# Last row block in quarter-width groups, with a variance about the first half's mean and one quarter centred on GpSimd

## What is computed

```python
def layer_norm(x, g, b):
    xf = x.astype(jnp.float32)
    mu = jnp.mean(xf, -1, keepdims=True)
    var = jnp.mean(jnp.square(xf - mu), -1, keepdims=True)
    y = (xf - mu) * lax.rsqrt(var + LN_EPS)
    return (y * g.astype(jnp.float32) + b.astype(jnp.float32)).astype(x.dtype)

x = layer_norm(ALPHA * x + 0.5 * swiglu(x, ffn_w_gate[l, 1], ffn_w_up[l, 1], ffn_w_down[l, 1]), ln_g[l, 3], ln_b[l, 3])
```

## Time and profile before

| | us |
|---|---|
| median of 3 runs | 1162.56 (1161.37 to 1162.63) |
| the profiled execution | 1161.91 |
| its span, first to last instruction | 1160.1 |
| PE busy in it | 1146.1 (99%) |
| DVE busy in it | 572.6 (49%) |
| ACT busy in it | 422.8 (36%) |
| POOL busy in it | 33.4 (3%) |

### The profile page before, as it was taken

The page is one execution under the profiler, slowest core; times in us unless marked ns, Lnnn a source line. Parts: engine busy times, 40 slices in busy tenths (PEclk is TensorE's granted clock), DMA queues, the critical chain, the costliest instruction groups (busy, mean ns, idle before and its releaser), DMA issues.

```text
span 1160.1 us, 14690 instructions
## 1 busy us (share of the span) xinstructions
PE 1146.1 (99%) x5454; PEld 955.7 (82%) x5454; DVE 572.6 (49%) x931; ACT 422.8 (36%) x690; POOL 33.4 (3%) x50
## 2 busy tenths in 40 slices
PE   8999999999999999999999999999999999999997
PEld 7888888888888888788898888889888888888885
DVE  4533333353338588764894765467333333343325
ACT  4412212232325377643463554345122122143222
POOL 2000000000001011000000000000000000000000
PEclk9999999999999999999999999999999999999999
DMA  7633223233222222342253341233322322332201
GB/s 256 239 94 103 93 93 104 92 110 108 91 90 73 91 71 82 99 150 73 73 166 108 106 149 55 73 109 128 106 93 90 103 96 90 102 116 91 97 30 73
DMA packets 33709, 120.86 MB, mean 104 GB/s; under 512 B 3917, under 2 KB 3933, under 8 KB 33409
## 3 DMA queue, kind: packets, MB, share of 16 engines
q1 hardware_dynamic: 30672, 109.07, 28.6%
q0 software_dynamic: 2992, 11.19, 2.8%
HBM read 118.13 MB, written 2.11 MB: 104 GB/s over the span
## 4 chain that ended last, share of the span: by engine, by line
PE 95%; DVE 3%; ACT 1%; issue 1%; DMA 0%; SPq 0%; DVEq 0%; ACTq 0%
PE ps L452 30%; PE ps L454 30%; PE ps L453 30%; PE ps L469 1%; PE ps L679 1%; PE ps L700 1%; PE ps L767 1%; DMA raw<-in_units 0%; PE ps L751 0%; DVE lg L1566 0%; PE ps L672 0%; PE ps L671 0%; PE ps L863 0%; DVE qs L1521 0%; ACT ew L927 0%
## 5 line engine op out<-in xcount | busy, mean ns | idle before, releaser
L1360 DVE TENSOR_TENSOR wlo<-raw,whi 128x1024 fp32r<-128x1024 f32 x196 | 239.7, 1227 | 372.2 <-ACT whi L927 371.3
L452 PE MATMUL ps<-xth,whi 128*128 128x512 f32 (+1 forms) x916 | 353.7, 386 | 1.7 <-DVE wlo L1492 1.7
L454 PE MATMUL ps<-xth,wlo 128*128 128x512 f32 (+1 forms) x916 | 351.6, 384 | 0.0
L453 PE MATMUL ps<-xtl,whi 128*128 128x512 f32 (+1 forms) x916 | 351.5, 384 | 0.0
L927 ACT ACTIVATE whi<-raw 128x1024 fp32r<-128x1024 f32 (+2 forms) x204 | 206.9, 1036 | 154.5 <-PE ps L454 141.8
L452 PEld LDWEIGHTS ps<-xth,whi 128*128 128x128 f32 x916 | 172.2, 188 | 35.1 <-DVE wlo L1492 2.2
L454 PEld LDWEIGHTS ps<-xth,wlo 128*128 128x128 f32 x916 | 172.1, 188 | 34.3
L453 PEld LDWEIGHTS ps<-xtl,whi 128*128 128x128 f32 x916 | 172.2, 188 | 32.9
L452 PE MATMUL ps<-whi,hhi 128*128 128x512 f32 x480 | 187.9, 391 | 0.7 <-DVE hlo L1367 0.7
L454 PE MATMUL ps<-whi,hlo 128*128 128x512 f32 x480 | 186.9, 389 | 0.0
L453 PE MATMUL ps<-wlo,hhi 128*128 128x512 f32 x480 | 186.8, 389 | 0.0
(11 more groups left out here) (186 smaller groups left out, 991.4 us busy)
## 6 DMA issues: line engine op xcount, KB each, us to landing
raw<-in_units SPq DMA_DIRECT2D x203, 512.0 KB, 3.3
gb<-in_ln_g POOLq DMA_DIRECT2D x4, 512.0 KB, 4.2
gb<-in_ln_b POOLq DMA_DIRECT2D x4, 512.0 KB, 5.4
xn<-in_x POOLq DMA_DIRECT2D x4, 512.0 KB, 12.6
wb<-in_bias_by_key POOLq DMA_DIRECT2D x8, 256.0 KB, 2.9
out<-xn SPq DMA_DIRECT2D x8, 256.0 KB, 2.0
gsp<-g_rows POOLq DMA_DIRECT2D x1, 1024.0 KB, 5.0
memn<-in_mem_cols POOLq DMA_DIRECT2D x1, 1024.0 KB, 5.6
```

The costliest lines, as they stand in the source:

```text
L452: mm(dst, lh, rh, start=start, stop=False)
L453: mm(dst, lh, rl, start=False, stop=False)
L454: return mm(dst, ll, rh, start=False, stop=stop)
L1360: v.tensor_tensor(wlo[c % SPL][:, :], raw[c % RAW][:, :], whi[c % SPL][:, :].bitcast(F32), ALU.subtract).then_inc(lo_done, 1)
```

## The change

Only the row block b = 3 of the last layer norm is treated anew; the blocks 0 to 2 of it, and all other layer norms, are as they were.

- TensorE: the last bank's closing twelve matmuls become twelve of columns 0 to 255 into `ps[7]` and then twelve of columns 256 to 511 into `ps[0]`, as a group of its own (its first 18 contraction tiles stay in `ps[7]`). Before the second group TensorE waits for the mean of row block 0.
- DVE (`norm_last`): the residual is added in the pieces 0 to 511, 512 to 767 and 768 to 1023, the last one twice, once with the part in `ps[7]`, once with that in `ps[0]`. From the first half's sum it makes a provisional mean. Small operations of 128 by 1 make the true mean and correct the variance by the square of the difference of the two means. `centered` is made by DVE in columns 0 to 767. The final step is in 640 and 384 columns; the second waits for GpSimd.
- ACT (`inv_std_last`): three Squares (512, 256 and 256 columns) about the provisional mean, then Ln and Exp.
- GpSimd: after the true mean, it makes `centered` in columns 768 to 1023 with two operations, an addition and a multiplication by the gains.
- SP: the last block's two stores are of 640 and 384 columns (320 and 192 KB).

```diff
@@ -19,6 +19,7 @@
 SPL = 6
 AHEAD = 4
 TAIL = 4
+POOL_COLS = 256
 PTS = 5
 SMALL = 6
 FFN_TILES = 22
@@ -156,6 +157,7 @@
         xsum = sb("xsum", [P, NB, 2])
         nmean = sb("nmean", [P, NB])
         sqsum = sb("sqsum", [P, NB])
+        fin = sb("fin", [P, 10])
         rstd = sb("rstd", [P, NB])
         eps_col = sb("eps_col", [P, 1])
 
@@ -264,6 +266,12 @@
         rstd_done = sem("rstd_done")
         ln_done = sem("ln_done")
         out_ready = sem("out_ready")
+        fin_mean_done = sem("fin_mean_done")
+        fin_sq_done = sem("fin_sq_done")
+        fin_row_done = sem("fin_row_done")
+        fin_var_done = sem("fin_var_done")
+        fin_nmean_done = sem("fin_nmean_done")
+        pool_cols_done = sem("pool_cols_done")
         xtr_done = sem("xtr_done")
         xhi_done = sem("xhi_done")
         xlo_done = sem("xlo_done")
@@ -362,7 +370,8 @@
                     load(c, i)
             for b in range(NB):
                 for h in range(2):
-                    c = slice(h * 512, h * 512 + 512)
+                    mid = 640 if b == NB - 1 else 512
+                    c = slice(mid, D) if h else slice(0, mid)
                     sp.wait_ge(out_ready, 2 * b + h + 1)
                     sp.dma_start(out[0, b * P:(b + 1) * P, c], xn[:, b, c]).then_inc(row_out, 16)
             sp.wait_ge(row_out, 16 * 2 * NB)
@@ -438,6 +447,15 @@
             load_gb(2)
             pool.wait_ge(ln_done, NB * 3)
             load_gb(3)
+            top, b = D - POOL_COLS, NB - 1
+            pool.wait_ge(gb_in, 32 * 4)
+            pool.wait_ge(fin_row_done, 2)
+            pool.wait_ge(fin_nmean_done, 1)
+            nc.gpsimd.tensor_scalar(centered[3][:, top:], xn[:, b, top:], nmean[:, b:b + 1], None, ALU.add)\
+                .then_inc(pool_step, 1)
+            pool.wait_ge(pool_step, 2)
+            nc.gpsimd.tensor_tensor(centered[3][:, top:], centered[3][:, top:], gb[:, 0, top:], ALU.mult)\
+                .then_inc(pool_cols_done, 1)
 
 
         @block.tensor
@@ -523,13 +541,13 @@
                         tile(f, i)
                 tile(FT - 1)
 
-            def product(n, k, b, start, stop, halves=(0, 1)):
+            def product(n, k, b, start, stop, halves=(0, 1), part=slice(0, 512), into=None):
 
                 u0, nk, h0 = DOWN[n]
                 u, s = u0 + k, (h0 + k) % SPL
                 for half in halves:
-                    c = slice(half * 512, half * 512 + 512)
-                    last = three(ps[2 * b + half][:, :], hhi[s][:, b * P:(b + 1) * P],
+                    c = slice(half * 512 + part.start, half * 512 + part.stop)
+                    last = three((into or ps[2 * b + half])[:, part], hhi[s][:, b * P:(b + 1) * P],
                                  hlo[s][:, b * P:(b + 1) * P], whi[u % SPL][:, c], wlo[u % SPL][:, c],
                                  start, stop)
                 return last
@@ -574,6 +592,15 @@
                 for b in range(NB):
                     for half in range(2):
                         end = b == NB - 1 and half == 1
+                        if end and n == 3:
+                            for k in range(nk - TAIL, nk):
+                                last = product(n, k, b, False, k == nk - 1, (half,), slice(0, 256))
+                            last.then_inc(acc_done, 1)
+                            pe.wait_ge(mean_done, NB * n + 1)
+                            for k in range(nk - TAIL, nk):
+                                last = product(n, k, b, k == nk - TAIL, k == nk - 1, (half,), slice(256, 512), ps[0])
+                                last.then_inc(unit_used, 1)
+                            continue
                         for k in range(nk - TAIL, nk):
                             if b == 0 and half == 0:
                                 need_both(n, k)
@@ -955,6 +982,23 @@
                 step.link(fn(rstd[:, b:b + 1], sqsum[:, b:b + 1], ACT.Ln, scale=1.0 / D, bias=eps_col[:, 0:1]))
                 fn(rstd[:, b:b + 1], rstd[:, b:b + 1], ACT.Exp, scale=-0.5).then_inc(rstd_done, 1)
 
+            def inv_std_last():
+
+                b = NB - 1
+                ends = (0, 512, 768, D)
+                for g in range(3):
+                    if g == 0:
+                        act.wait_ge(fin_mean_done, 1)
+                    else:
+                        act.wait_ge(fin_row_done, g)
+                    c = slice(ends[g], ends[g + 1])
+                    fn(squares[3][:, c], xn[:, b, c], ACT.Square, scale=D ** -0.5, bias=fin[:, 3:4],
+                       accum_out=fin[:, 4 + g:5 + g]).then_inc(fin_sq_done, 1)
+                act.wait_ge(fin_sq_done, 3)
+                act.wait_ge(fin_var_done, 1)
+                step.link(fn(rstd[:, b:b + 1], fin[:, 9:10], ACT.Ln, scale=-1.0, bias=fin[:, 6:7]))
+                fn(rstd[:, b:b + 1], rstd[:, b:b + 1], ACT.Exp, scale=-0.5).then_inc(rstd_done, 1)
+
             def h_tile(n, k, i=None):
 
                 if i is None:
@@ -1031,8 +1075,10 @@
                     x_hi(n + 1, 1)
                 split(ut + AHEAD + 2)
                 split(ut + AHEAD + 3)
-                inv_std(n, 3)
-                if n < 3:
+                if n == 3:
+                    inv_std_last()
+                else:
+                    inv_std(n, 3)
                     x_hi(n + 1, 2)
 
 
@@ -1403,6 +1449,52 @@
                         v.scalar_tensor_tensor(out=xn[:, b, c], in0=centered[n][:, c], scalar=rstd[:, b:b + 1],
                                                in1=gb[:, 1, c], op0=ALU.mult, op1=ALU.add).then_inc(out_ready, 1)
 
+            def norm_last():
+
+                b = NB - 1
+                ends = (0, 512, 768, D)
+                top = D - POOL_COLS
+
+                def rows_in(g, bank, scalar=ALPHA):
+                    c = slice(ends[g], ends[g + 1])
+                    return v.scalar_tensor_tensor(out=xn[:, b, c], in0=xn[:, b, c], scalar=scalar,
+                                                  in1=bank[:, c.start % 512:(c.stop - 1) % 512 + 1],
+                                                  op0=ALU.mult, op1=ALU.add, accum_out=fin[:, g:g + 1])
+
+                dve.wait_ge(acc_done, (2 * NB - 1) * 3 + 2 * b + 1)
+                step.link(rows_in(0, ps[2 * b]))
+                v.tensor_scalar(fin[:, 3:4], fin[:, 0:1], -(D ** -0.5) / 512, None, ALU.mult).then_inc(fin_mean_done, 1)
+                dve.wait_ge(acc_done, (2 * NB - 1) * 3 + 2 * b + 2)
+                rows_in(1, ps[2 * b + 1]).then_inc(fin_row_done, 1)
+                step.link(rows_in(2, ps[2 * b + 1]))
+                dve.wait_ge(fin_row_done, 1)
+                step.link(v.tensor_scalar(fin[:, 7:8], fin[:, 0:1], fin[:, 1:2], -1.0 / D, ALU.add, ALU.mult))
+                dve.wait_ge(fin_mean_done, 1)
+                step.link(v.scalar_tensor_tensor(out=fin[:, 8:9], in0=fin[:, 3:4], scalar=-(D ** 0.5), in1=fin[:, 7:8],
+                                                 op0=ALU.mult, op1=ALU.add))
+                dve.wait_ge(fin_sq_done, 2)
+                step.link(v.tensor_scalar(fin[:, 4:5], fin[:, 4:5], fin[:, 5:6], LN_EPS, ALU.add, ALU.add))
+                dve.wait_ge(gb_in, 32 * 4)
+                dve.wait_ge(unit_used, DOWN[3][0] + DOWN[3][1])
+                rows_in(2, ps[0], 1.0).then_inc(fin_row_done, 1)
+                dve.wait_ge(fin_row_done, 2)
+                v.scalar_tensor_tensor(out=nmean[:, b:b + 1], in0=fin[:, 2:3], scalar=-1.0 / D, in1=fin[:, 7:8],
+                                       op0=ALU.mult, op1=ALU.add).then_inc(fin_nmean_done, 1)
+                step.link(v.scalar_tensor_tensor(out=fin[:, 8:9], in0=fin[:, 2:3], scalar=-1.0 / D, in1=fin[:, 8:9],
+                                                 op0=ALU.mult, op1=ALU.add))
+                v.scalar_tensor_tensor(out=fin[:, 9:10], in0=fin[:, 8:9], scalar=fin[:, 8:9], in1=fin[:, 4:5],
+                                       op0=ALU.mult, op1=ALU.subtract).then_inc(fin_var_done, 1)
+                dve.wait_ge(fin_nmean_done, 1)
+                step.link(v.scalar_tensor_tensor(out=centered[3][:, 0:top], in0=xn[:, b, 0:top],
+                                                 scalar=nmean[:, b:b + 1], in1=gb[:, 0, 0:top],
+                                                 op0=ALU.add, op1=ALU.mult))
+                dve.wait_ge(rstd_done, NB * 4)
+                for c in (slice(0, 640), slice(640, D)):
+                    if c.stop == D:
+                        dve.wait_ge(pool_cols_done, 1)
+                    v.scalar_tensor_tensor(out=xn[:, b, c], in0=centered[3][:, c], scalar=rstd[:, b:b + 1],
+                                           in1=gb[:, 1, c], op0=ALU.mult, op1=ALU.add).then_inc(out_ready, 1)
+
             def split_h(n, k, i=None):
                 src = hb[n][:, k * S:(k + 1) * S] if i is None else hb[n][:, bass.ds(k * S + i * (SPL * S), S)]
                 split_act(3 * n, k, src, i)
@@ -1473,8 +1565,10 @@
                     x_lo(n + 1, 1)
                 split(ut + AHEAD + 2)
```

(6 more changed lines are left out.)

## The result

The changed kernel takes 1178.68 us (median of 4 runs, 1177.01 to 1179.45) against 1161.99 for the kernel before (median of 4 in the same comparison): ratio 1.0141, 95% interval 1.0127 to 1.0154, 16.7 us slower. I had forecast 1164.1 us and given 0.86 to no change that can be told; the time lies far above the range. The profiled execution took 1178.51 us, its span is 1176.3, 16.2 more than before.

What follows compares the result with a forecast made beforehand. The prediction took TensorE's matmul stream to bound the body, with only the tail's chain through DVE and ACT able to move. Later xn, GpSimd holds and stores summed to +1.5 us on 1162.56: 1164.1 us, range 1162.3 to 1165.4.

Steps and rivals of the forecast that it cites:

- The step that failed: Kernel body: a matmul stream, TensorE 95% of the 1160.1 us span, untouched by the diff before its last twelve matmuls.
- 0.86 for no change: Whole kernel: chance that the measured time lies within about 0.2%, 2.3 us, of the kernel before.
- PE's end: TensorE's closing matmuls: twenty-four of 256 columns, a start every 0.120 us, ending at 1152.27, 0.15 later than before.
- xn finished: DVE's additions in the last row block: xn done at 1154.14 instead of 1152.85, 1.29 later.
- My price of 0.11 for two waits: DVE's small operations in the tail: an instruction behind two semaphore waits starts 0.11 us after its releaser.
- a brake that I had ruled out: DVE's sum of the squares: ACT would not delay it, two squares being done at 1153.20, before its start at 1153.33.
- DVE held by GpSimd: DVE after xn: POOL's SBUF operations hold the variance, `centered` and the final step; DVE ends at 1157.93, 1.47 later.
- the direction that I had called an inference: Tail's SBUF access: POOL also waits for DVE, its multiplication, ready at 1155.05, starting only at 1155.91.
- rivals 2 and 3: Tail: `centered` precedes POOL's addition, final step's second part waits for POOL; +1.75, 22%, or with dearer operations +2.5, 12%.
- rival 2: Tail: `centered` gets in before POOL's addition, final step's second part waits for POOL's multiplication; +1.75, 1164.3 us, 22%.
- The stores: SP's last two stores: the last issued about 1157.96 instead of 1156.49, shifting the end by 1.3 to 1.6, taken as 1.5.
- The tail's sum: From the last row block to the span's end: +1.5 us, span 1161.6, 1164.1 by the median; forecast keeps 43%.

Runs made afterwards that it cites:

- both sweeps: Two kernels without the layer, only matmuls at chosen operand offsets: groups of 24, one execution 336.44 us; finer offsets and narrower matmuls, groups of 48, 328.32 us.

## Why the prediction was wrong, step by step

**The step that failed** is the first: that the body is a matmul stream "and the diff does not touch it before its last twelve matmuls". I had read the diff for instructions. Its line for `fin` adds no instruction and moves one operand of over 4300 matmuls of 512 columns. The levels of the table account for the loss, roughly: 2604 matmuls at +0.0026 and 1716 in the changed kernel at +0.0066 us make 18.1 us, against 16.46 measured. By the means over the whole trace (0.2270 to 0.2292 us for the 2604, 0.2270 to 0.2333 for the 1716) it is 16.5 us, so the surplus was the coarse reading of eleven starts. The last paragraph of the prediction did say that a time above 1165.5 would mean that something outside the tail had moved, and so it was, but with no chance given to it. The 0.86 for no change fits the tail and was wrong about the kernel: with `fin` out of the way the ratio is 1.0000. It fits the tail for other reasons than I gave, which is luck: DVE's end came later through a wait that the forecast did not have, and the stores did not follow DVE.

**The tail**, in DVE's queue after the change (timeline of DVE, from the second small operation on):

```profile
1168.99 0.21 DVE L1471 TENSOR_SCALAR fin<-fin 128x1 f32<-128x1 f32 x1
1169.24 0.16 DVE L1473 SCALAR_TENSOR_TENSOR fin<-fin 128x1 f32<-128x1 f32 x1
1169.73 0.21 DVE L1476 TENSOR_SCALAR fin<-fin 128x1 f32<-128x1 f32 x1 [0.33 <-ACT squares L954]
1169.98 0.42 DVE L1460 SCALAR_TENSOR_TENSOR xn<-xn,ps 128x256 f32<-128x256 f32 x1
1170.33 0.08 DVE L1460 DVE_READ_ACCUMULATOR xn<-xn,ps 128x1 f32 x1
...
1170.71 0.22 DVE L1485 SCALAR_TENSOR_TENSOR fin<-fin 128x1 f32<-128x1 f32 x1
1170.85 1.01 DVE L1488 SCALAR_TENSOR_TENSOR centered<-xn,nmean,gb 128x768 f32<-128x768 f32 x1
1171.89 0.90 DVE L1495 SCALAR_TENSOR_TENSOR xn<-centered,rstd,gb 128x640 f32<-128x640 f32 x1
1173.41 0.62 DVE L1495 SCALAR_TENSOR_TENSOR xn<-centered,rstd,gb 128x384 f32<-128x384 f32 x1 [0.62 <-POOL centered L457]
```

- *PE's end.* Twenty-four matmuls of 256 columns, forecast 0.120 us a start from the earlier trace rows. With `fin` at the end it is 0.120 (1147.91 to 1150.55 in 22 steps). In the changed kernel it was 0.114 (1165.78 to 1168.40 in 23 steps): at this width the shift helps. I had put the 0.120 down to a weight load that is not fully hidden; that is not enough, for the load of 128 by 128 takes 0.19 us in both kernels and only the operands' places differ. Neither matters, since DVE was already late, as forecast.
- *xn finished* 3.01 us after the first addition began, forecast 3.20, before 1.91. The direction and most of the size were right: the queue of small operations costs more than the narrower last addition gives. My price of 0.11 for two waits was too high: with the first met by a neighbour on the same engine they cost 0.03 to 0.04 (1168.96 to 1168.99). Because DVE was early by that, it did wait for ACT, 0.33 us, a brake that I had ruled out; the last addition, which needs nothing of ACT, stood behind it. It began 1.3 us after PE's end, forecast 1.4. The forecast has small slips here (1151.85 and 0.42 make 1152.27, not 1152.24), and DVE had not one gap up to PE's end but a second of 0.56 before 1149.61; neither changes the result.
- *DVE held by GpSimd.* Forecast: the variance, `centered` and the final step held, DVE's end 1.47 later. Measured: none was held; `centered` took its plain 1.01. DVE was first by 0.1 us (variance at 1170.71, POOL at 1170.82), and GpSimd was held instead:

```profile
1170.82 1.75 POOL L454 TENSOR_SCALAR centered<-xn,nmean 128x256 f32<-128x256 f32 x1 [361.73 <-DVE nmean L1481]
1172.65 0.72 POOL L457 TENSOR_TENSOR centered<-centered,gb 128x256 f32<-128x256 f32 x1
```

  Together with its 0.93 alone this is the row that the trace of before lacked, a GpSimd operation waiting for DVE. Here the Trainium skill ("SBUF — State Buffer", section "Who interferes with whom") and the trace agree, on the direction that I had called an inference. But the first part of the final step, 0.90 us with both inputs in SBUF, ran beside the addition's last 0.7 us nearly at its plain duration (0.885 in the three traces in which GpSimd had nothing left to do), so a hold of a whole operation on each side isn't what these rows show; this stays open.
- *The second part of the final step* waited 0.62 us for GpSimd, at the place that rivals 2 and 3 had named: DVE got ahead of GpSimd's addition as in rival 2, not behind it as in the forecast. DVE's end came 6.62 us after the first addition, 1.10 more than the 5.52 of before; forecast 1.47, rival 2 1.75.
- *The stores.* From DVE's end to the span's end there were 3.64 us before and 2.32 after, so 1.32 come back; I had let them follow DVE's shift. The changed kernel's last two stores, us to landing:

```profile
out<-xn SPq DMA_DIRECT2D x1, 320.0 KB, 2.2
out<-xn SPq DMA_DIRECT2D x1, 192.0 KB, 1.9
```

  Against 3.2 us for the last one before. The 0.62 us of waiting for GpSimd set the last store apart from the first (the two issues together span 1.57 us instead of 0.99) and it is smaller. With 320 and 192 KB and issues spanning 0.86 us (no GpSimd) it was 2.63 us; with two of 256 KB, issued 0.66 us apart each time, it was 3.64, 3.63 and 3.64 in three traces (the kernel before, hhi and hlo by 64, the arena by 64) and 2.89 in two others (the kernel before with 64 and with 192 bytes of padding). Why those two differ is not known. Against them only 0.57 come back, and size and distance were never changed one at a time, so what the new stores are worth stays open.
- *The tail's sum*: +1.10 - 1.32 = -0.22 us against the kernel before, forecast +1.5. The sign is not shown: against the kernel before with the same 64 bytes of padding, whose stretch is 8.57 us, the changed kernel's 8.94 is 0.4 us longer. The measured ratio with `fin` at the end, 1.0000 with 0.0009 to either side, allows any of the values from -1.0 to +1.0, and excludes the 1.5.

## What to carry to other kernels

Read a diff for what it allocates before what it executes: in a kernel bound by TensorE, a 64-byte tile in the middle of the layout cost 16 us of 1162, while the change that it served moved the time by less than the 1 us that the runs can tell. Put new small tiles behind the large ones, or keep the moving and the stationary operands of the frequent matmuls at the same place modulo 256 bytes (measured here for 512 columns; at 256 columns another place is best), and look at the distance between matmul starts, not at their duration, when a body slows without idle time. And a tail whose engine is already late gains nothing from finer pieces: here the added small operations, the second pass over a quarter of the columns and the waits for ScalarE and GpSimd put DVE's end 1.10 us later.

## What the runs showed of the hardware

- A float32r matmul of 512 columns with its stationary operand loaded anew each time starts every 0.227 us when both operands start at the same place modulo 256 bytes of a partition, and every 0.229, 0.232 and 0.233 us when the moving one lies 64, 128 or 192 bytes behind; 0.238 at 4 bytes (11.40 us for 48, start to marker). With both moved together by multiples of 64 bytes nothing changes (5.51 to 5.53 us for 24 at eight places), but at a difference of 16 bytes it matters which operand was moved (11.18 against 11.03 us for 48). The granted clock was 1.00 of full speed in both sweeps and in the stretches compared, and the recorded duration of a matmul stays 0.39. That the loading of the next stationary operand and the streaming of the current moving one meet somewhere would explain that the difference counts; no run separated the two, so this is argued, not shown. The Trainium skill ("SBUF — State Buffer", section "Who interferes with whom") lists TensorE's two reads, moving operand and weight load, as independent; the time of these runs depends on their relative place.
- At 256 columns the order of the places is different: 192 bytes is the fastest (0.115 against 0.121 us), at 384 three of the places take 8.38 us for 48 and 128 bytes takes 8.50.
- GpSimd's addition of a per-row scalar to 128 by 256 elements took 0.93 us alone, in one trace, dearer than its two-input multiplication of the same size, 0.72, and 1.75 in the four traces in which DVE's `centered` ran beside it.
